# A three-layer fp32 block on one core: where layer 1's convolution, key chains and gates stand among the attention units

## The chip, the cores and the metric

One Trainium2 chip, one core. The time is device microseconds of one launch, the median over the runs. All arithmetic is fp32; in the third layer it is fp32 split into two fp32r parts.

## The reference, cut to what matters

Sequence 256, model width 1024, 256 memory tokens. An even layer (0), an odd layer (1) and a third layer of another kind, which the change doesn't touch. Layer 1:

```python
h = rms_norm(x, norm_g)
c_a, c_b, c_g, d_q, d_kv, d_bg, d_g, m_q, m_g = split_cols(h @ w_in, ODD_SPLITS)
# conformer_conv: 31 taps per channel over 512 channels, causal
y = conv(pad(c_a * sigmoid(c_b))) + conv_b
y_c = silu(rms_norm(y, c_norm)) * silu(c_g)
# nsa: 8 heads; each softmax(q k) v over 15 compressed keys ("cmp"),
# over the selected blocks ("slc") and over the window ("win"), weighted by gates
kc = rope(rms_norm(compress(k_cmp_raw), knorm))     # 15 keys, an MLP over 32 tokens each
y_d = nsa(d_q, kv, gates, ...) * silu(d_g)
# memory_attention: 4 heads over 256 memory tokens, q and k normed
y_m = memory_attention(m_q, mem_n, m_wkv, ...) * silu(m_g)
x = x + concat([y_c, y_d, y_m]) @ w_out
```

Layer 0 has the same memory attention, an 8-head differential attention (two softmaxes a head) and a gated unit, with q and k normed per group and turned by rope.

## The kernel before, in words

The kernel writes each engine's instruction stream by hand; each stream is executed in order, and engines meet at semaphores. TensorE (PE) does projections, transposes, scores and values. ScalarE (ACT) copies projections out of PSUM, does exp and tanh, and copies turned probabilities out. VectorE (DVE) does norms, rope, masks, row maxima, the scaling of probabilities, and most of the convolution. GpSimd (POOL) does the power of each norm (L1905, one small instruction per norm, in the order of the list `NORMS`), one of the four channel tiles of the convolution, and in the third layer the low parts of the weights (L1873). SyncE loads weights in the order of `WHOLE`, five slots deep.

A projection of 512 columns (`project`, L452) has two halves; each fills one of two PSUM banks (the ring `proj`). Transposes go through another two banks (the ring `xpose`), in the order of `xpose_names`; a turn waits until the bank's last content has been copied out.

Attention is cut into units, one softmax of one head over all 256 queries: layer 0 has 20 (4 memory, 16 differential), layer 1 has 28 (4 memory, then cmp, slc, win for each of 8 heads). `layer_units` is a software pipeline with the same iteration i on every engine. TensorE: scores of unit i+1 (L558), some steps of the "fill" projections (L452), turn of unit i-1 (L568), values of unit i-2 (L575). VectorE: logits and row minimum of unit i (`unit_logits`, L1411 to L1421), probabilities of unit i-1 (`unit_probs`, L1428 to L1434), finished fill pieces, and then `extra(i)`. ScalarE: exp of unit i, tanh of a fill piece, copy of unit i-1.

The fill of layer 1 is `L1_FILL = ["c_b", "c_a", "c_g", "d_g"]`, 64 steps spread over the 28 units. So the convolution's input is there only at about unit 14. From then on VectorE does 6 taps of the convolution at the end of every iteration (3 channel tiles x 2 taps, L1608 and L1610; only every third waits for its result) and GpSimd 31 taps of the fourth tile (L1884 to L1888, a product and a sum each). After the last unit come, in order: the last taps, bias (L1629), transposes (L748), the turns of `ym1` and of `yb1` (from y_d), `out_rest` (the output projection's last 256 rows) and the first part of `out_project`, then the turn of `ya1` (from y_c), the rest, and the residual. The norm of y_c and its gate run beside `out_rest`.

Ahead of the units, layer 1 projects `d_q`, `dkv1`, `dkv2`, runs the 128 small matmuls of the compression (L691), projects `m_qg1`, and then goes through two short chains with every engine in turn: hidden layer, `kvc`, norm and rope of the compressed keys, `kc`; and norm and turn of the memory queries (`mq1`).

Of the kernel before, what the change touches and what calls it, by code (L numbers as in the profile page):

```python
# [10 lines left out]
ALU = mybir.AluOpType  # L11
# [52 lines left out]
L1_FILL = ["c_b", "c_a", "c_g", "d_g"]  # L64
# [7 lines left out]
def both(names):  # L72
# [4 lines left out]
WHOLE = (both(["kv0", "b_q", "b_k", "m_qg0", "b_v"] + L0_FILL) + out_halves(0)  # L77
         + both(["kv1", "d_q", "dkv1", "dkv2", "cmp_w1", "m_qg1"] + L1_FILL) + out_halves(1))
# [94 lines left out]
FILL_MM = 4 * T * KT  # L173


def fill_after(i, n):

    return min(FILL_MM, FILL_MM * (i + 1) // n)


def pieces_at(i, n):

    before = fill_after(i - 1, n) // KT if i else 0
    return range(before, fill_after(i, n) // KT)


def xpose_names():
    out = [f"mem{j}" for j in range(4)] + [f"x0_{j}" for j in range(4)]
    out += ["mk0", "q0", "q1", "k0", "k1", "mq0"]
    out += [("unit", i) for i in range(len(UNITS0))]  # L190
    out += ["z0", "z1", "ym0", "ya0_0", "ya0_1", "yb0_0", "yb0_1"]
    out += [f"x1_{j}" for j in range(4)] + ["cmp", "dq0", "dq1", "hid_k", "hid_v", "mk1", "dk0", "dk1", "hid_t", "kvc", "kc", "mq1"]
    out += [("unit", len(UNITS0) + i) for i in range(len(UNITS1))]
    out += ["yc0", "yc1", "ym1", "yb1_0", "yb1_1", "ya1_0", "ya1_1"]
    out += [f"x2_{j}" for j in range(4)] + ["rq0", "rq1", "rk0", "rk1"] + [("ret", h) for h in range(RET_HEADS)]
    out += [f"ret_y{j}" for j in range(4)] + [f"x3_{j}" for j in range(4)]
    return out


def proj_names():  # L200
    out = []
    for b in ["kv0", "b_q", "b_k", "m_qg0", "b_v"] + L0_FILL + ["out0"] + \
# [11 lines left out]
def build(nc, early_d, late_d, positions_d, x_d, mem_d, blocks_d, out_d):  # L214
# [5 lines left out]
    with ExitStack() as ctx:  # L220
# [62 lines left out]
        kc_rows = logits[:, 1, 0:256].rearrange("p (g c d) -> p g c d", g=2, d=64)  # L283
# [18 lines left out]
        def pair_of(c0, i):  # L302
# [30 lines left out]
        normed = Milestones(sem("normed"), ["mem", "x0", "mk0", "q", "k", "mq0", "a_v", "y_m0", "y_a0", "y_b",  # L333
                                               "x1", "dq", "mk1", "dk", "hid", "kc", "mq1", "conv", "y_m1",
                                               "y_d", "y_c", "x2", "rq", "rk", "g_ret", "x3"])
        NORMS = [("mem", 2), ("x0", 2), ("mk0", 8), ("q", 32), ("k", 32), ("mq0", 8), ("a_v", 8),
                 ("y_b", 16), ("x1", 2), ("dq", 16), ("mk1", 8), ("dk", 8), ("kc", 2), ("mq1", 8), ("y_c", 2), ("x2", 2), ("gn0", 4), ("gn1", 4),
# [8 lines left out]
                              [(1, "tanh", p) for p in range(4, 8)])  # L346
# [42 lines left out]
        def slot_left(eng, part):  # L389
            if part > 0:  # L390
                last = max(j for j in whole_done if j % WHOLE_SLOTS == part - 1)
                eng.wait_ge(*whole_done[last])
            else:
                eng.wait_ge(*whole_done[whole_index[("kv1", 1)]])
# [15 lines left out]
        CONV_FROM = 1 + max(i for i in range(len(UNITS1)) if 3 in pieces_at(i, len(UNITS1)))  # L410
        CONV_VECTOR, CONV_POOL = (0, 1, 2), 3
# [8 lines left out]
        def _(pe):  # L420
# [75 lines left out]

            def turn_pair(name, tiles):
# [9 lines left out]
            def out_rest(layer):  # L507
# [5 lines left out]
                for c in range(4):  # L513
# [3 lines left out]
                    for t in range(T):  # L517
                        for k in range(2):
                            mm = products(psum[:, bank + ring.slot(use), t * HC:(t + 1) * HC],
                                          pick(h_whole, slice(None), k, slice(t * P, (t + 1) * P)),  # L520
# [70 lines left out]
            turned(pe, "x0_2", "x0_3")  # L591
            project("b_q", h_whole)
            normed.wait(pe, "mk0")
            turn_pair("mk0", lambda a, t: mkv[:, 0, t, a * P:(a + 1) * P])
            project("b_k", h_whole)
# [3 lines left out]
            project("m_qg0", h_whole)  # L599
            normed.wait(pe, "k")  # L600
            for j in range(2):
                turn_pair(f"k{j}", lambda a, t: rows[:, t, 2048 + (2 * j + a) * P:2048 + (2 * j + a + 1) * P])
            project("b_v", h_whole)
            normed.wait(pe, "mq0")
            turn_pair("mq0", lambda a, t: rows[:, t, 3584 + a * P:3584 + (a + 1) * P])
            turned(pe, "k0", "k1", "mq0")
            turned(pe, "q0", "q1", "mk0")
            chunk_read(pe, "b_v")
# [12 lines left out]
            def layer_units(units, base, operands, fill, group_starts):  # L621
                filler = (s for name in fill for t in range(T)
                          for s in (features_piece if name in ("c_a", "c_b") else rows_piece)(name, t, h_whole))
# [4 lines left out]
                for i in range(n + 2):  # L628
                    if i + 1 < n:
                        unit_scores(base + i + 1, units[i + 1], *operands(units[i + 1])[0:2])  # L630
                    while issued < fill_after(i, n):
# [4 lines left out]
                    if i >= 2:  # L636
                        if i - 2 in group_starts:
                            heads_out.wait(pe, group_starts[i - 2])
                        unit_values(base + i - 2, units[i - 2], *operands(units[i - 2])[2:])
                for _ in filler:  # L640
                    pass


            layer_units(UNITS0, 0, operands0, L0_FILL, {4: "mem0"})
# [35 lines left out]
            for j in range(2):  # L680
                turn_pair(f"dq{j}", lambda a, t: rows[:, t, (2 * j + a) * P:(2 * j + a + 1) * P])
            project("dkv2", h_whole, (HC, 24))
            src_full.wait(pe, "cmp")
# [14 lines left out]
            normed.wait(pe, "mk1")  # L698
            turn_pair("mk1", lambda a, t: mkv[:, 1, t, a * P:(a + 1) * P])
            normed.wait(pe, "dk")  # L700
            for j in range(2):
                turn_pair(f"dk{j}", lambda a, t: rows[:, t, 3072 + (2 * j + a) * P:3072 + (2 * j + a + 1) * P])
            project("m_qg1", h_whole)
# [6 lines left out]
            turned(pe, "hid_t")  # L710
            xpose.claim(pe, "kvc")
            for c in range(2):
                for g in range(2):
                    at = (2 * c + g) * 64
                    mm = nc.tensor.matmul(psum[0:N_CMP, XPOSE_BANK + xpose.slot("kvc"), at:at + 64],
                                          hid[:, c, g * N_CMP:(g + 1) * N_CMP], E("cmp_w2")[:, c * 64:(c + 1) * 64],
                                          start=True, stop=True)
            fill(xpose, mm, "kvc")
            normed.wait(pe, "kc")
            xpose.claim(pe, "kc")  # L720
            for g in range(2):
                mm = nc.tensor.transpose(psum[:, XPOSE_BANK + xpose.slot("kc"), g * 16:(g + 1) * 16],
                                         kc_rows[0:16, g].rearrange("p a d -> p (a d)"), ident[0:16, 0:16])
            fill(xpose, mm, "kc")
            normed.wait(pe, "mq1")
            turn_pair("mq1", lambda a, t: rows[:, t, 1536 + a * P:1536 + (a + 1) * P])
            turned(pe, "dq0", "dq1", "mk1", "dk0", "dk1", "kc", "mq1")
# [15 lines left out]
            layer_units(UNITS1, len(UNITS0), operands1, L1_FILL, {0: "diff", 4: "mem1"})  # L743
            normed.wait(pe, "conv")
            for t in range(T):
                xpose.claim(pe, f"yc{t}")
                for f in range(4):
                    mm = nc.tensor.transpose(psum[:, XPOSE_BANK + xpose.slot(f"yc{t}"), f * P:(f + 1) * P],  # L748
                                             conv_out[:, f, t * P:(t + 1) * P], ident)
                fill(xpose, mm, f"yc{t}")  # L750
            normed.wait(pe, "y_m1")
            turn_pair("ym1", lambda a, t: rows[:, t, 1792 + a * P:1792 + (a + 1) * P])
            normed.wait(pe, "y_d")
            for j in range(2):
                turn_pair(f"yb1_{j}", lambda a, t: rows[:, t, 2560 + (2 * j + a) * P:2560 + (2 * j + a + 1) * P])
# [8 lines left out]

            def project_features(name, src):
                for half in range(2):
                    for _ in features_piece(name, half, src):
                        pass
# [127 lines left out]
        def _(act):  # L896
# [119 lines left out]
            act.wait_ge(lam_exp, 1)  # L1016
            copy_chunk("b_q", rows[:, :, 1536:2048])
            copy_chunk("b_k", rows[:, :, 2048:2560])
            copy_chunk("m_qg0", rows[:, :, 3584:4096])

            gate_m.mark(nc.scalar.activation(gate_tmp[:, :, :], rows[:, :, 3840:4096], ACT.Tanh, scale=0.5), 0, act)
            copy_chunk("b_v", rows[:, :, 2560:3072])

            def fill_half(layer, p, name, gelu):

                arrive(proj, name)
                if layer == 1 and p < 2:

                    proj.freed(nc.scalar.activation(rows[:, p, 3584:4096], bank_of(name),
                                                    ACT.Tanh, scale=0.5), name, act)  # L1030
                    return
                if layer == 1 and p < 4:
                    return
# [998 lines left out]
```

## Time and profile before

| | us |
|---|---|
| median of 3 runs | 1113.35 (1112.9 to 1115.66) |
| the profiled execution | 1114.8 |
| its span | 1113.0 |
| PE busy | 962.0 (86%) |
| DVE busy | 465.6 (42%) |
| ACT busy | 362.1 (33%) |
| POOL busy | 537.6 (48%) |

Layer 0's first score is at 98.47 us of the span, layer 1's first score at 353.68, and layer 1's output projection begins at 511.45; the third layer's work takes the rest from about 564. A row of a timeline gives start, duration, engine, line, operation, out<-in, shapes, the number of merged instructions, and in brackets the idle time before it and who ended it.

### The profile page before, as it was taken

Reading aid. Unit: us, or ns where it says so; the run is one execution under the profiler, and the core shown is the slowest. Engines: PE = TensorE matmul, PEld = TensorE weight load, DVE = VectorE, ACT = ScalarE, POOL = GpSimd, SP = SyncE. Lnnn points to the kernel's source line nnn. Section 1 sums busy time; section 2 is a strip of 40 time slices with the busy share of each in tenths; the row PEclk is TensorE's granted clock in tenths of the full one; section 3 lists DMA queues with packets and bytes.
Section 4 is the critical chain, followed back from the end, with each engine's and each line's share of the span. In section 5 each row is a group of like instructions: output and inputs, shape, how many; then the busy total and the mean of one; then the engine's idle time right before and its main releaser. Section 6 shows DMA issues by size and latency. Waiting matters only on the chain.

```text
span 1113.0 us, 15392 instructions
## 1 busy us (share of the span) xinstructions
PE 962.0 (86%) x5960; PEld 864.6 (78%) x5960; DVE 465.6 (42%) x965; ACT 362.1 (33%) x641; POOL 537.6 (48%) x710
## 2 busy tenths in 40 slices
PE   4999799999995996878789887769998699999995
PEld 3888578788884874657689877669998699899994
DVE  1454545421334459985189330560113236222231
ACT  2212333301001432222144474524433434334441
POOL 0030000000110029400469949379889578999993
PEclk9999899999997997797989898979999799999998
DMA  8343122233442221132234434135454335555551
GB/s 324 124 143 116 73 76 76 77 125 140 151 152 76 76 76 39 39 113 90 67 99 149 143 112 152 61 108 187 156 171 152 114 133 170 172 186 178 185 181 47
DMA packets 37608, 139.36 MB, mean 125 GB/s; under 512 B 4256, under 2 KB 4256, under 8 KB 37280
## 3 DMA queue, kind: packets, MB, share of 16 engines
q1 hardware_dynamic: 37392, 136.97, 36.2%
q10 hardware_dynamic: 144, 1.41, 0.3%
q8 instruction: 47, 0.77, 0.3%
q14 instruction: 25, 0.20, 0.1%
HBM read 137.32 MB, written 1.05 MB: 124 GB/s over the span
## 4 chain that ended last, share of the span: by engine, by line
PE 21%; POOL 19%; DVE 5%; ACT 4%; issue 1%; DVEq 0%; ACTq 0%; POOLq 0%
POOL w_lo L1873 18%; PE psum L453 7%; PE psum L454 7%; PE psum L455 7%; DVE y_lo L1276 1%; ACT w_hi L910 1%; DVE h_lo L1250 0%; PE psum L504 0%; DVE h_rows L1752 0%; ACT act_tmp L966 0%; POOL rstd L1905 0%; ACT h_hi L933 0%; ACT y_hi L961 0%; ACT rows L1148 0%; ACT rows L1146 0%
## 5 line engine op out<-in xcount | busy, mean ns | idle before, releaser
L1873 POOL TENSOR_TENSOR w_lo<-raw,w_hi 128x256 fp32r<-128x256 f32 x624 | 460.0, 779 | 106.5 <-ACT w_hi L910 65.4
L452 PE MATMUL psum<-w_whole,h_whole 128*128 128x256 f32 (+1 forms) x960 | 224.3, 391 | 2.2 <-ACT h_whole L945 2.2
L1905 POOL TENSOR_TENSOR rstd<-mean_sq,minus_half 128x2 f32<-128x2 f32 (+4 forms) x20 | 34.1, 1704 | 395.0 <-DVE mean_sq L1288 395.0
L453 PE MATMUL psum<-h_hi,w_hi 128*128 128x256 f32 x704 | 204.8, 291 | 20.8 <-POOL w_lo L1873 16.7
L452 PEld LDWEIGHTS psum<-w_whole,h_whole 128*128 128x128 f32 x960 | 183.1, 197 | 37.2 <-issue 10.2
L454 PE MATMUL psum<-h_lo,w_hi 128*128 128x256 f32 x704 | 203.6, 289 | 0.0
L455 PE MATMUL psum<-h_hi,w_lo 128*128 128x256 f32 x704 | 203.3, 289 | 0.0
L910 ACT ACTIVATE w_hi<-raw 128x1024 fp32r<-128x1024 f32 x156 | 159.0, 1054 | 108.3 <-DMA raw<-in_blocks 63.8
L453 PEld LDWEIGHTS psum<-h_hi,w_hi 128*128 128x128 f32 x704 | 139.8, 199 | 23.2 <-issue 18.3
L454 PEld LDWEIGHTS psum<-h_lo,w_hi 128*128 128x128 f32 x704 | 140.0, 199 | 0.0
L455 PEld LDWEIGHTS psum<-h_hi,w_lo 128*128 128x128 f32 x704 | 139.7, 198 | 0.0
L984 ACT ACTIVATE logits<-logits,neg_max 128x128 f32<-128x128 f32 (+2 forms) x96 | 41.4, 431 | 93.1 <-DVE neg_max L1421 57.0
L453 PE MATMUL psum<-w_hi,h_hi 128*128 128x256 f32 x192 | 56.7, 295 | 12.4 <-DVE rows L1770 6.2
L453 PE MATMUL psum<-w_hi,y_hi 128*128 128x512 f32 (+1 forms) x160 | 56.8, 355 | 4.3 <-DVE y_lo L1276 3.6
L452 PE MATMUL psum<-w_whole,y_whole 128*128 128x256 f32 x256 | 56.1, 380 | 1.9 <-DVE y_whole L1259 1.9
L568 PE MATMUL psum<-early,logits 128*128 128x128 f32 (+1 forms) x144 | 26.3, 294 | 35.5 <-DVE logits L1434 35.4
L454 PE MATMUL psum<-w_lo,y_hi 128*128 128x512 f32 (+1 forms) x160 | 56.3, 352 | 0.0
L455 PE MATMUL psum<-w_hi,y_lo 128*128 128x512 f32 (+1 forms) x160 | 56.2, 351 | 0.0
L454 PE MATMUL psum<-w_lo,h_hi 128*128 128x256 f32 x192 | 56.0, 292 | 0.0
L455 PE MATMUL psum<-w_hi,h_lo 128*128 128x256 f32 x192 | 55.9, 291 | 0.0
L452 PEld LDWEIGHTS psum<-w_whole,y_whole 128*128 128x128 f32 x256 | 48.5, 190 | 8.8 <-ACT y_whole L942 2.3
L568 PEld LDWEIGHTS psum<-early,logits 128*128 128x128 f32 (+1 forms) x144 | 17.6, 144 | 46.5 <-DVE logits L1434 43.0
(264 smaller groups left out, 1421.4 us busy)
## 6 DMA issues: line engine op xcount, KB each, us to landing
raw<-in_blocks SPq DMA_DIRECT2D x156, 512.0 KB, 3.4
w_whole<-in_blocks SPq DMA_DIRECT2D x96, 512.0 KB, 4.4
early<-in_early SPq DMA_DIRECT2D x1, 1647.0 KB, 8.4
attention<-in_late ACTq DMA_DIRECT2D x1, 1380.0 KB, 5.8
rows<-in_mem SPq DMA_DIRECT2D x1, 1024.0 KB, 4.9
x<-in_x SPq DMA_DIRECT2D x1, 1024.0 KB, 10.5
out_x<-h_rows SPq DMA_DIRECT2D x1, 1024.0 KB, 4.0
positions<-in_positions SPq DMA_DIRECT2D x1, 1.0 KB, 10.2
```

Source lines behind the costliest of these rows:

```text
L452: return nc.tensor.matmul(out, lhs[0], rhs[0], start=start, stop=stop, skip_group_check=shared_bank)
L453: nc.tensor.matmul(out, lhs[0], rhs[0], start=start, stop=False, skip_group_check=shared_bank)
L454: nc.tensor.matmul(out, lhs[0], rhs[1], start=False, stop=False, skip_group_check=shared_bank)
L455: return nc.tensor.matmul(out, lhs[1], rhs[0], start=False, stop=stop, skip_group_check=shared_bank)
L568: mm = nc.tensor.transpose(bank[0:rows_, n * P:(n + 1) * P], logits[:, i % 3, u.cols(t, kb)], ident)
L910: nc.scalar.activation(split_part(w_hi, q), raw[:, q % RAW_SLOTS, :], ACT.Copy).then_inc(w_hi_ready, 1)
L984: ins = nc.scalar.activation(logits[:, i % 3, u.seg(t)], logits[:, i % 3, u.seg(t)], ACT.Exp, bias=neg_max[:, i % 2, t:t + 1], scale=-1.0, ...
L1276: src_lo.mark(V.tensor_tensor(pair[1][at], src, pair[0][at].bitcast(F32), ALU.subtract), name, vec)
L1873: ins = nc.gpsimd.tensor_tensor(lo[:, at], full[:, at], hi[:, at].bitcast(F32), ALU.subtract)
L1905: rstd_ready.mark(nc.gpsimd.tensor_tensor(rstd[:, n % 2, 0:width], mean_sq[:, n % 2, 0:width], minus_half[:, 0:width], ALU.pow), name, pool)
```

## The change

- **Layer 0.** `m_qg0` is projected first, the memory queries are normed and turned ahead of b_q, and the turns of k (`k0`, `k1`) move from ahead of the units into iteration 1.
- **Layer 1, order.** `c_b` and `c_a` leave the fill and are projected ahead of `dkv2`; `m_qg1` comes ahead of the compression. `L1_FILL` is `c_g` and `d_g`, 32 steps, spread over 27 units.
- **Convolution.** VectorE has two tiles (1, 3) in place of three, one after the other, each tap waiting for the one before; 24 taps ahead of the units, 3 per iteration from iteration 3. GpSimd has two tiles (0, 2): 20 taps ahead of the power of `mq1`, 6 ahead of that of `kc`, the other 36 ahead of that of `y_c`.
- **Key chain.** `kvc`, the norm of the compressed keys and `kc` move into iterations 1 and 2.
- **End of y_c.** Bias in iteration 17, transposes in 18, norm in 19, tanh in 20, gate in 21, turns of `ym1` and `ya1` in 22. After the units only y_d is left; `out_project` begins with the rows of y_c.

```diff
-L1_FILL = ["c_b", "c_a", "c_g", "d_g"]
+L1_FILL = ["c_g", "d_g"]
+CONV_END = 17
+FILL_UNITS = [20, 27]
-    out += ["mk0", "q0", "q1", "k0", "k1", "mq0"]
-    out += [("unit", i) for i in range(len(UNITS0))]
+    out += ["mk0", "mq0", "q0", "q1", ("unit", 0), "k0", "k1"]
+    out += [("unit", i) for i in range(1, len(UNITS0))]
-            ["kv1", "d_q", "dkv1", "dkv2", "m_qg1"] + L1_FILL + ["out1"] + \
+            ["kv1", "d_q", "dkv1", "c_b", "c_a", "dkv2", "m_qg1"] + L1_FILL + ["out1"] + \
-        CONV_VECTOR, CONV_POOL = (0, 1, 2), 3
+        CONV_VECTOR, CONV_POOL = (1, 3), (0, 2)
...
# TensorE, layer 1
+            project_features("c_b", h_whole)
+            normed.wait(pe, "mk1")
+            turn_pair("mk1", ...)
+            normed.wait(pe, "dk")
+            for j in range(2):
+                turn_pair(f"dk{j}", ...)
+            project_features("c_a", h_whole)
             project("dkv2", h_whole, (HC, 24))
+            project("m_qg1", h_whole)
             src_full.wait(pe, "cmp")
...
+            normed.wait(pe, "mq1")
+            turn_pair("mq1", ...)
             normed.wait(pe, "hid")
...
+            def between_units(i):
+                if i == 1:
+                    turned(pe, "hid_t")
+                    xpose.claim(pe, "kvc")
...
+                elif i == 2:
+                    normed.wait(pe, "kc")
...
+                    turned(pe, "kc")
+                elif i == CONV_END + 1:
+                    normed.wait(pe, "conv")
...
+                elif i == CONV_END + 5:
+                    normed.wait(pe, "y_c")
+                    turn_pair("ym1", ...)
+                    for j in range(2):
+                        turn_pair(f"ya1_{j}", ...)
             out_rest(1)
-            turned(pe, "yb1_0", "yb1_1")
-            out_project(1, range(4, 8), lambda: turn_last(3584, "y_c", ("ya1_0", "ya1_1")))
+            turned(pe, "ya1_0", "ya1_1")
+            out_project(1, range(0, 4), lambda: turn_last(2560, "y_d", ("yb1_0", "yb1_1")))
# VectorE, layer 1: each half of c_a, then 8 taps; later, ahead of the hidden layer, 8 more
+            for half in range(2):
...
+                proj.freed(ins, ("c_a", half), vec)
+                taps(8)
...
+            normed.mark(grouped_norm("mq1", heads(rows, 1536, 4, 64), E("m1_qnorm")), "mq1", vec)
...
+            taps(8)
             for j, name in enumerate("kv"):
                 arrive(xpose, f"hid_{name}")
...
             def extra1(i):
+                if 3 <= i < CONV_END:
+                    taps(3)
+                if i == 1:
+                    arrive(xpose, "kvc")
...
+                elif i == CONV_END:
+                    taps(2 * 31)
+                    vec.wait_ge(conv_sums, len(CONV_POOL))
...
+                elif i == CONV_END + 2:
+                    grouped_norm("y_c", yc, E("c_norm")).then_inc(yc_normed, 1)
...
# GpSimd
+                for half, f in enumerate(CONV_POOL):
+                    proj.read(pool, ("c_a", half))
+                    for tap in range(31):
...
+            taps_ahead = {"mq1": 20, "kc": 6, "y_c": 2 * 31}
             for n, (name, width) in enumerate(NORMS):
-                if name == "y_c":
...
+                for _ in range(taps_ahead.get(name, 0)):
+                    next(conv, None)
```

## Rows read from the trace of the kernel before

**Rows 1.** Busy time of the engines by stretch: width, busy time (instructions), granted clock

```profile
353.60:410.90 57.30, 57.22 (x305) 46.92 (x306) 26.58 (x91) 21.35 (x73) 0.00 (x0) 0.95 0.18 57
410.90:458.90 48.00, 34.01 (x139) 25.17 (x137) 45.73 (x82) 9.35 (x34) 43.23 (x61) 0.82 0.14 48
458.90:500.00 41.10, 31.21 (x152) 24.11 (x153) 36.39 (x105) 11.94 (x41) 0.00 (x0) 0.90 0.25 89
500.00:511.40 11.40, 7.92 (x35) 6.93 (x35) 8.02 (x17) 2.67 (x5) 0.00 (x0) 0.50 0.31 124
```

**Rows 2.** TensorE timeline at the start of layer 0's units

```profile
96.86 0.60 PE L504 MATMUL psum<-early,rows 128*128 128x128 f32 x4
98.47 1.14 PE L558 MATMUL psum<-attention 64*128 64x256 f32 x8 [1.00 <-DVE attention L1330]
```

**Rows 3.** TensorE timeline ahead of layer 1's units

```profile
303.83 10.56 PE L452 MATMUL psum<-w_whole,h_whole 128*128 128x256 f32 x64
314.31 8.87 PE L691 MATMUL psum<-w_whole,h_rows 64*30 64x128 f32 x128
326.06 13.98 PE L452 MATMUL psum<-w_whole,h_whole 128*128 128x256 f32 x64
...
345.90 0.39 PE L722 MATMUL psum<-early,logits 16*128 16x16 f32 x2 [4.28 <-DVE logits L1573]
350.93 1.12 PE L504 MATMUL psum<-early,rows 128*128 128x128 f32 x4 [4.63 <-DVE rows L1304]
353.68 2.08 PE L558 MATMUL psum<-attention 64*128 64x256 f32 x8 [1.63 <-DVE attention L1330]
```

**Rows 4.** GpSimd timeline, layer 1: norms, first and last convolution instruction

```profile
347.64 1.64 POOL L1905 TENSOR_TENSOR rstd<-mean_sq,minus_half 128x8 f32<-128x8 f32 x1 [3.84 <-DVE mean_sq L1288]
410.92 0.61 POOL L1884 TENSOR_TENSOR h_rows<-rows,early 128x256 f32<-128x256 f32 x1 [61.64 <-DVE rows L1594]
...
458.13 0.72 POOL L1888 TENSOR_TENSOR h_rows<-h_rows,rope_tmp 128x256 f32<-128x256 f32 x1
```

**Rows 5.** VectorE convolution taps by form: without GpSimd, then beside it

```profile
L1610 DVE SCALAR_TENSOR_TENSOR h_rows<-rows,early,h_rows 128x256 f32<-128x256 f32 x6 | 2.6, 481 | 0.1
...
L1610 DVE SCALAR_TENSOR_TENSOR h_rows<-rows,early,h_rows 128x256 f32<-128x256 f32 x6 | 4.8, 847 | 0.1
```

**Rows 6.** VectorE timeline: starts of iterations 15, 18, 21 and 24

```profile
417.95 0.56 DVE L1414 SCALAR_TENSOR_TENSOR logits<-psum,early 128x384 f32<-128x384 f32 x1
...
441.71 0.56 DVE L1414 SCALAR_TENSOR_TENSOR logits<-psum,early 128x384 f32<-128x384 f32 x1
...
463.25 0.56 DVE L1414 SCALAR_TENSOR_TENSOR logits<-psum,early 128x384 f32<-128x384 f32 x1
...
477.03 0.56 DVE L1414 SCALAR_TENSOR_TENSOR logits<-psum,early 128x384 f32<-128x384 f32 x1
```

**Rows 7.** TensorE timeline: turns of units 7 and 10

```profile
386.24 0.49 PE L568 MATMUL psum<-early,logits 128*128 128x128 f32 x3
...
397.81 0.49 PE L568 MATMUL psum<-early,logits 128*128 128x128 f32 x3
```

**Rows 8.** VectorE timeline: compressed keys and memory queries

```profile
341.74 0.41 DVE L1566 TENSOR_SCALAR kvc<-psum 15x256 f32<-15x256 f32 x1 [0.79 <-PE psum L715]
...
345.38 0.22 DVE L1572 COPY logits<-kvc 15x128 f32<-15x128 f32 x1
...
347.33 0.17 DVE L1288 TENSOR_SCALAR mean_sq<-sumsq 128x8 f32<-128x8 f32 x1
```

**Rows 9.** VectorE and TensorE timeline after the last unit

```profile
503.68 1.14 DVE L1629 TENSOR_SCALAR h_rows<-h_rows,early 128x256 f32<-128x256 f32 x4
...
512.49 1.23 DVE L1297 TENSOR_TENSOR scratch<-rows 128x1024 f32<-128x1024 f32 x1
...
517.33 1.29 DVE L1304 SCALAR_TENSOR_TENSOR rows<-rows,early 128x512 f32<-128x512 f32 x2
...
511.45 7.56 PE L452 MATMUL psum<-w_whole,h_whole 128*128 128x256 f32 x32
```

More of the change, by code:

```diff
@@ L73, in both @@
     return [(n, h) for n in names for h in range(2)]
[L77 to L78 removed]
+WHOLE = (both(["kv0", "m_qg0", "b_q", "b_k", "b_v"] + L0_FILL) + out_halves(0)
+         + both(["kv1", "d_q", "dkv1", "c_b", "c_a", "dkv2", "m_qg1", "cmp_w1"] + L1_FILL) + out_halves(1))
 HALVES = (both(["x_lru0", "x_lru1", "r_q", "r_k", "y_lru0", "y_lru1", "lru_w", "r_v0", "r_v1", "g_ret0", "g_ret1"]
@@ L598, in _ @@
                 turn_pair(f"q{j}", lambda a, t: rows[:, t, 1536 + (2 * j + a) * P:1536 + (2 * j + a + 1) * P])
[L599 to L602, printed above, removed]
             project("b_v", h_whole)
[L604 to L608, printed above, removed]
+            turned(pe, "mk0", "mq0", "q0", "q1")
             chunk_read(pe, "kv0")
@@ L619, in operands0, with layer_units @@
                         u.sub == 0, u.sub == 1)
-            def layer_units(units, base, operands, fill, group_starts):
-                filler = (s for name in fill for t in range(T)
-                          for s in (features_piece if name in ("c_a", "c_b") else rows_piece)(name, t, h_whole))
+            def layer_units(layer, units, base, operands, fill, group_starts, extra=lambda i: None):
+                filler = (s for name in fill for t in range(T) for s in rows_piece(name, t, h_whole))
                 n = len(units)
@@ L697, in _ @@
                 ends(("cmp_w1", half), *full_value(xpose, "hid_v"))
[L698 to L703, printed above, removed]
+            normed.wait(pe, "mq1")
+            turn_pair("mq1", lambda a, t: rows[:, t, 1536 + a * P:1536 + (a + 1) * P])
             normed.wait(pe, "hid")
@@ L709, in _ @@
             fill(xpose, mm, "hid_t")
[L710 to L727, printed above, removed]
+            turned(pe, "dq0", "dq1", "mk1", "dk0", "dk1", "mq1")
             chunk_read(pe, "kv1")
@@ L1046, in fill_tanh, with layer_units @@
                               (layer, "tanh", p), act)
-            def layer_units(layer, units, base, fill, groups):
+            def layer_units(layer, units, base, fill, groups, extra=lambda i: None):
                 n = len(units)
@@ L1083, in _ @@
             copy_chunk("dkv1", rows[:, :, 512:1024])
+            for half in range(2):
+                arrive(proj, ("c_b", half))
+                proj.freed(nc.scalar.activation(rows[:, half, 3584:4096], bank_of(("c_b", half)), ACT.Tanh, scale=0.5),
+                           ("c_b", half), act)
             copy_chunk("dkv2", rows[:, :, 1024:1304], (HC, 24))
@@ L1558, in _ @@
             normed.mark(V.memset(lam_tmp[:, 7:8], 0.0), "hid", vec)
-            turn_in("mk1", mk_t[:, 1])
-            for j in range(2):
-                turn_in(f"dk{j}", k_t[:, 2 * j:2 * j + 2, :])
+            turn_in("mq1", mq_t[:, :, :])
             arrive(xpose, "hid_t")
```

334 lines of the change are left out of this document (177 added, 157 removed).

## The prediction, before the changed kernel ran

> **What bounds the kernel now.** I read the page's chain of waits first: it stays in the third layer, which the change doesn't touch and which waits for the second residual, so whatever layers 0 and 1 gain or lose passes on to the end. Then busy time by stretch [rows 1]. From 353.6 to 410.9 TensorE has no idle time (57.2 of 57.3 us at clock 0.95): it bounds. From 410.9 to 458.9 VectorE is busy 45.7 of 48.0 us and TensorE 34.0 at a granted clock of 0.82: VectorE bounds, since convolution taps stand in every iteration. Up to 500 VectorE still leads (36.4 of 41.1), and from 500 to 511.4 short transposes follow the last unit at clock 0.50. The change puts work and waits of these last two stretches elsewhere, and takes on the 10.5 us of waits ahead of the units (4.28, 4.63 and 1.63) [rows 3].
>
> Two prices from VectorE decide. A tap lasts 481 ns with GpSimd idle, and six go by in 2.6 us; beside GpSimd's taps it lasts 847 ns, and six take 4.8, that is 0.81 each [rows 5]. GpSimd does 31 taps in 47.9 us, 1.55 each [rows 4]: two instructions per tap, so one VectorE tap per GpSimd instruction. Three iterations with 18 taps take 23.8 us beside GpSimd (417.95 to 441.71) and 13.8 without (463.25 to 477.03) [rows 6]. Without the taps (14.5 and 7.8 us) and one fill piece (0.9, in the first only), three iterations cost VectorE 8.4 us beside GpSimd and 5.9 without.
>
> **Layer 0.** TensorE waits 1.00 us for the memory queries after a 0.60 turn [rows 2]; with q, k and mq in the new order VectorE's k norm ends with `b_v`, and I get the first score at 97.1 in place of 98.5. The two k turns (2 x 0.5) come back in iteration 1, and `k1` needs the bank that ScalarE has to empty of unit 0 (about 0.6). Net +0.3, bounds -1.4 and +2.
>
> **Layer 1 up to the units.** c_b starts where `dkv2` did, at 303.8. TensorE then runs 13.98 (c_b), 2.0 (mk1 and dk turns), 13.98 (c_a), 10.5 (dkv2), 13.98 (m_qg1), 8.9 (compression) [rows 3]: it ends at 367.0. c_a's first half is there at 326.8, GpSimd starts at 328.1 and has 20 taps by 359.1, in time for `mq1`, whose sums are ready at 360.8 (m_qg1 ends at 358.1). GpSimd's power takes 1.64 [rows 4], so 362.7; then GpSimd starts 6 more taps. VectorE finishes norm and gate, slowed by them, at 366.7, and now has 8 taps ahead of the hidden layer: 6.5 us, 373.2. TensorE's turn of `mq1` wants the bank of `hid_k`, which VectorE frees behind those taps: TensorE idles from 367.0 to about 373.4, and wakes on the low clock. From the `mq1` turn to the first score took 2.75 us before (350.93 to 353.68) [rows 3]: first score at 376.1, +22.4. So of 28 us of projections moved ahead, 5.6 are paid by waits that went; a new wait of 6 us replaced the rest.
>
> **Iterations 0 to 3.** Two of them begin as before (logits 0 at 378.2, probabilities 0 done at 382.0). Iteration 1 then has the whole key chain inside VectorE's stream: 4.1 us before (341.7 to 345.8) [rows 8], with a memset 4.4, and once GpSimd has its power it resumes the last 36 taps (at 385.8) and the small two-input operations behind it wait for its instructions, some eight times 0.3: 391. Unit 1's turn and `kc` wait for that; iteration 2 ends at 396, iteration 3 with its 3 taps at 400.9. Before, iteration 4 began at 367.5: the shift is now +33.4.
>
> **Iterations 4 to 16.** GpSimd ends at 385.8 + 36 x 1.55 = 441.9. Beside it an iteration costs 8.4/3 + 3 x 0.81 = 5.2 us (before: 6 taps, 7.6); 40.1 us without one piece give 7.7 of them. TensorE's own work is 2.9: three units took 11.57 [rows 7], of which 28 instructions of fill at 13.98/64 = 0.218 (6.1 us), so 1.8 a unit, and 1.0 of fill now. The remaining 4.3 iterations with taps cost 2.0 + 3 x 0.52 = 3.5 (each tap now waits for the one before, so 481 ns and an issue of 35): with one piece, iteration 16 begins at 457.3, iteration 17 at 458.8. Before, it began at 433.1: +25.7.
>
> **Iteration 17 to the output projection.** Bias 1.1 [rows 9]; VectorE waits about 2 for the transposes and copies 1.4; the norm of y_c is 6.2 in one piece (512.49 to 518.6 [rows 9]), in iteration 19, in which TensorE idles some 5 us; gate 2.5; the three turns of iteration 22 cost VectorE about 4 us of waiting, because three bank uses are emptied one by one. Eleven iterations of VectorE's 1.97 make 21.6, its y_c work 11.9, two pieces 1.6, and the waits about 14 (2 and 4 above, 5 in iterations 24 to 27 where TensorE's 2.9 bounds, 3 for the last values): 49.4. `out_rest` starts at 508.2, not 511.45: -3.3. It no longer needs y_d, whose product and copy (3 us) lie under 14 us of matmuls, as y_c's gate did.
>
> **Sum.** +0.3 - 3.3 = -3.0 on a span of 1113.0. The profiled execution took 1114.8, above the median of 1113.35; I take the difference off the median: **1110.4**. The third layer is the same work from the residual on. `late` loads earlier, hidden; the weights' queue keeps its five slots, and its last loads wait for fill that ends at 500 and are needed after 535.
>
> **GpSimd's lock.** On the traces GpSimd loses little to VectorE: 1.55 a tap with VectorE busy 45.7 of 48 us [rows 1, 4]. The Trainium skill (SBUF — State Buffer, Who interferes with whom) says that a VectorE instruction with two SBUF inputs and a GpSimd instruction that reads SBUF hold the shared pair for the whole instruction, and the other fully blocks. By this rule, GpSimd would lose a tap's whole 0.48 each time too; the sum without the rule stands above, and what it would do is the third rival.
>
> **Rivals.**
> - *Lighter contention (faster).* With two tiles each, VectorE's taps fall between GpSimd's instructions and cost 0.52, the lower bound of rows 5. Then the hidden layer comes 2.4 us earlier, an iteration beside GpSimd costs 4.3, 9.3 fit instead of 7.7, worth 5.6 us: 1102. For it speaks that a tap with nothing beside it needs only that; against it, that beside GpSimd all six taps of a row pay 0.81.
> - *Each tap misses a turn (slower).* All of VectorE's taps now wait for the one before; before, two in three didn't. If a tap that comes late lets GpSimd through again, it costs up to two GpSimd instructions, 1.55. The taps ahead of the hidden layer cost 6 more, an iteration 7.4, so 5.4 fit and 2.3 more run at 3.5 (+8): 1125. The gain is gone at 0.95 a tap and the kernel slower by 0.3% at 1.1. Against: a GpSimd instruction of 0.6 to 0.8 is much longer than the 35 ns of issue.
> - *GpSimd is held up (slower).* If VectorE's two-input operations block it fully, about 1.8 of each 5.2 us, its 36 taps take 85 us: they end at 471, VectorE waits in iteration 17, and the end is 12 later: 1123.
> - *The wait only moves (no change).* TensorE at clock 0.8 or below has 5.5 us of work per iteration at the low level against VectorE's 5.2; three idle stretches of 5 us or more each bring that level. 3 us lost so: 1113.
>
> **Numbers.** Chances: the forecast 0.50 (its own range 1106 to 1115), lighter contention 0.17, missed turns 0.12, GpSimd held up 0.05, the wait only moves 0.16. What this kernel's measurement can tell from no change is about 0.3%, 3.3 us; 1110.4 lies just inside it. The forecast's half splits 0.27 faster, 0.21 same, 0.02 slower. With the rivals: faster 0.44, same 0.37, slower 0.19. Range: 1102 from the lighter contention to 1120, between the forecast and the two slow rivals.
>
> **What the changed profile would show.** First score of layer 0 near 97.1. A hole in TensorE of about 6 us ahead of the `mq1` turn, ended by VectorE; first score of layer 1 near 376. VectorE's taps at about 0.85 until GpSimd's last one near 442, and 0.48 after; iterations of 5.2 and 3.5 us. No wait of VectorE for GpSimd in iteration 17. A TensorE hole of 5 us in iteration 20. `out_rest` at 508, then 37 us as before. I am wrong if taps cost another price, if GpSimd ends later than 455, or if TensorE's low clock makes it the bound beside GpSimd.

## The result, and the profile after

The changed kernel took 1127.7 us (median of 4, 1125.7 to 1129.0) against 1114.3 for the kernel before (4 runs beside it): a ratio of 1.0116, 95% interval 1.010 to 1.0131. It is slower by 1.2%, 13 us; I had forecast 1110.4, and 1120 was the upper end. The profiled execution took 1125.7, its span is 1123.9 (before: 1113.0), so the rows below hold 10.9 us of the loss.

Busy time by stretch of the changed kernel, the columns as in [rows 1]. The columns are start and end, width, then busy time with instructions of TensorE, of its weight loads, of VectorE, ScalarE and GpSimd, then TensorE's granted clock (1.00 is 2.4 GHz, 0.50 is 1.2 GHz), the DMA engines' busy share and GB/s. The stretches run from the first score to iteration 4, to GpSimd's last tap, to iteration 17, to the end of TensorE's wait for y_c's norm, through the three turns, to `out_rest`.

```profile
375.60:402.60 27.00, 18.00 (x74) 13.61 (x74) 17.95 (x36) 6.16 (x19) 16.34 (x25) 0.63 0.00 1
402.60:439.60 37.00, 31.60 (x118) 23.36 (x118) 34.57 (x68) 10.09 (x37) 33.31 (x48) 0.64 0.08 29
439.60:462.60 23.00, 20.66 (x96) 15.60 (x94) 18.67 (x57) 8.63 (x31) 0.61 (x1) 0.80 0.13 47
462.60:484.00 21.40, 15.48 (x82) 11.94 (x83) 14.69 (x39) 5.30 (x19) 0.71 (x1) 0.90 0.15 50
484.00:499.50 15.50, 15.19 (x61) 11.83 (x61) 7.13 (x17) 6.07 (x17) 0.00 (x0) 0.61 0.00 0
499.50:518.30 18.80, 14.74 (x88) 12.14 (x87) 10.65 (x39) 7.94 (x27) 0.00 (x0) 0.95 0.35 130
```

Two things stand out. Before, TensorE had no idle time in the 57 us after its first score, at clock 0.95 [rows 1]. Now it idles 9.0 of the first 27 us, and its granted clock is 0.63 (between the 1.2 and the 2.4 GHz level, nearer the lower). And from 484 to 499.5 it is busy all the time (15.19 of 15.5) at 0.61: there the clock itself costs time.

TensorE's timeline of the changed kernel: the first scores of both layers, the three places in layer 1 where it idled over 4 us, and `out_rest`; these answer to [rows 2, 3, 9]:

```profile
95.56 1.14 PE L566 MATMUL psum<-attention 64*128 64x256 f32 x8 [0.45 <-DVE q_t L1350]
...
373.24 1.09 PE L512 MATMUL psum<-early,rows 128*128 128x128 f32 x4 [8.00 <-DVE scratch L1623]
375.66 2.08 PE L566 MATMUL psum<-attention 64*128 64x256 f32 x8 [0.98 <-DVE hid L1629]
...
393.46 1.11 PE L576 MATMUL psum<-early,logits 128*128 128x128 f32 x4 [8.36 <-DVE logits L1458]
...
483.97 0.59 PE L576 MATMUL psum<-early,logits 128*16 128x128 f32 x2 [5.19 <-DVE logits L1458]
...
518.29 9.62 PE L455 MATMUL psum<-w_whole,mem_t 128*128 128x256 f32 x32
```

All three holes end with VectorE. Its timeline shows with what it was busy: the 8 taps; the key chain (its first instruction, two of its small two-input ones, and its last, a copy); its wait for the turn of `kc`; then iteration 4, the first after GpSimd's last tap, and iteration 17 (in iteration 11, three taps in 1.53 us):

```profile
366.36 6.42 DVE L1587 SCALAR_TENSOR_TENSOR h_rows<-rows,early,h_rows 128x256 f32<-128x256 f32 x8
...
383.09 0.41 DVE L1642 TENSOR_SCALAR kvc<-psum 15x256 f32<-15x256 f32 x1 [1.45 <-PE psum L751]
...
387.47 0.70 DVE L1338 TENSOR_TENSOR scratch<-kvc,early 15x16 f32<-15x16 f32 x1
388.21 0.16 DVE L1339 TENSOR_TENSOR kvc<-scratch 15x16 f32<-15x16 f32 x1
...
389.77 0.65 DVE L1651 COPY scratch<-kvc 15x128 f32<-15x128 f32 x1
...
396.60 0.19 DVE L1654 COPY kc_t<-psum 128x32 f32<-128x32 f32 x1 [3.20 <-PE psum L759]
...
402.64 0.19 DVE L1438 SCALAR_TENSOR_TENSOR logits<-psum,early 128x32 f32<-128x32 f32 x1
...
440.52 0.56 DVE L1438 SCALAR_TENSOR_TENSOR logits<-psum,early 128x384 f32<-128x384 f32 x1
...
442.64 1.53 DVE L1587 SCALAR_TENSOR_TENSOR h_rows<-rows,early,h_rows 128x256 f32<-128x256 f32 x3
...
462.63 0.56 DVE L1438 SCALAR_TENSOR_TENSOR logits<-psum,early 128x384 f32<-128x384 f32 x1 [1.30 <-issue]
```

VectorE itself waits in the stretch behind: for the transposes of y_c, for the three turns of iteration 22, and for the tanh of the last fill piece:

```profile
472.74 1.42 DVE L1670 COPY rows<-psum 128x512 f32<-128x512 f32 x2 [2.75 <-PE psum L768]
...
498.80 0.69 DVE L1279 TENSOR_SCALAR y_whole<-psum 128x512 f32<-128x512 f32 x1 [6.89 <-PE psum L512]
...
511.60 0.69 DVE L1471 SCALAR_TENSOR_TENSOR rows<-act_tmp,psum 128x512 f32<-128x512 f32 x1 [3.40 <-ACT act_tmp L1052]
```

GpSimd: end of its taps ahead of the keys' power, the power, its last tap; these answer to [rows 4]:

```profile
371.72 0.78 POOL L1929 TENSOR_TENSOR h_rows<-h_rows,rope_tmp 128x256 f32<-128x256 f32 x1
384.46 0.71 POOL L1943 TENSOR_TENSOR rstd<-mean_sq,minus_half 128x2 f32<-128x2 f32 x1 [11.96 <-DVE mean_sq L1308]
...
439.42 0.79 POOL L1931 TENSOR_TENSOR h_rows<-h_rows,rope_tmp 128x256 f32<-128x256 f32 x1
```

### The profile page after: what moved, and what is told of

The parts are those of the page before. It is cut to its first block and busy times, and to the rows that moved or that the text cites. A ratio compares the mean times of both kernels' runs of the same rounds, so it can differ in the third digit from the quotient of the medians.

```text
span 1123.9 us, 15419 instructions
## 1 busy us (share of the span) xinstructions
PE 974.5 (87%) x5960; PEld 873.8 (78%) x5960; DVE 461.7 (41%) x934; ACT 362.3 (32%) x641; POOL 580.2 (52%) x771
## 5 line engine op out<-in xcount | busy, mean ns | idle before, releaser
L455 PE MATMUL psum<-w_whole,h_whole 128*128 128x256 f32 (+1 forms) x928 | 228.0, 403 | 2.2 <-ACT h_whole L963 2.2
L455 PEld LDWEIGHTS psum<-w_whole,h_whole 128*128 128x128 f32 x928 | 180.3, 202 | 41.8 <-issue 15.0
L576 PE MATMUL psum<-early,logits 128*128 128x128 f32 (+1 forms) x144 | 28.7, 316 | 38.4 <-DVE logits L1458 38.3
L994 ACT ACTIVATE rows<-psum 128x512 f32<-128x512 f32 (+1 forms) x24 | 13.9, 580 | 130.6 <-PE psum L455 110.4
## 6 DMA issues: line engine op xcount, KB each, us to landing
positions<-in_positions SPq DMA_DIRECT2D x1, 1.0 KB, 10.1
```

Source lines behind the costliest of these rows:

```text
L455: return nc.tensor.matmul(out, lhs[0], rhs[0], start=start, stop=stop, skip_group_check=shared_bank)
L576: mm = nc.tensor.transpose(bank[0:rows_, n * P:(n + 1) * P], logits[:, i % 3, u.cols(t, kb)], ident)
L994: proj.freed(nc.scalar.activation(dst[:, :, c], bank_of((name, half)).rearrange("p (t n) -> p t n", t=T)[:, :, 0:cols[half]], ACT.Copy), ( ...
```

## The experiments

**Theory A:** the loss is VectorE work put where TensorE has nothing else left: the 8 taps ahead of the hidden layer, the key chain in iteration 1, the norm of y_c in iteration 19. **Theory B:** the contention between VectorE's and GpSimd's taps, each of which runs longer while the other engine works. **Theory C:** TensorE's low clock.

| run | us, median | ratio to before, 95% interval |
|---|---|---|
| the change | 1127.7 | 1.0116 (1.0100 to 1.0131) |
| layer 0's part alone | 1113.7 | 0.9990 (0.9977 to 1.0004) |
| y_c's end behind the units | 1119.9 | 1.0037 (1.0020 to 1.0055) |
| GpSimd's taps left out | 1114.1 | 0.9996 (0.9984 to 1.0009) |
| idle matmuls added | 1124.2 | 1.0086 (1.0067 to 1.0105) |
| 8 taps away from the hidden layer | 1119.5 | 1.0052 (1.0033 to 1.0071) |
| keys ahead of the units | 1123.9 | 1.0091 (1.0067 to 1.0115) |
| y_c's end and the 8 taps, both | 1111.6 | 0.9972 (0.9960 to 0.9983) |
| kernel before, tiles split 2 and 2 | 1117.3 | 1.0035 (1.0021 to 1.0049) |
| reordered | 1106.0 | 0.9929 (0.9912 to 0.9947) |
| reordered, more taps ahead | 1100.3 | 0.9856 (0.9840 to 0.9872) |
| the same with idle matmuls | 1100.8 | 0.9873 (0.9859 to 0.9886) |

Differences between runs are taken from the ratios, times 1114.3; by the intervals such a difference is uncertain by 2 to 3 us. Starts in a trace vary as well: the changed kernel and its variants share their layer 0, and yet layer 1's first projection starts between 302.33 and 305.86 us (302.39 in the changed kernel). Where starts of two traces are compared below, that difference is taken off.

**Layer 0's part alone**, on the kernel before:

```diff
-    out += ["mk0", "q0", "q1", "k0", "k1", "mq0"]
-    out += [("unit", i) for i in range(len(UNITS0))]
+    out += ["mk0", "mq0", "q0", "q1", ("unit", 0), "k0", "k1"]
+    out += [("unit", i) for i in range(1, len(UNITS0))]
```

> The kernel before with the layer 0 part alone. In the changed kernel's trace layer 0's first score came 2.9 us earlier, two thirds of it were lost again in iteration 1, and layer 1 began 1.4 us earlier. Every theory of the loss puts it in layer 1, so here the time should be 1 to 2 us below that of the kernel before (ratio 0.998 to 1.000). If it is above 1.002, part of the 13 us comes from layer 0.

1.1 us faster, and the interval holds no change as well: layer 0 has no part in the loss.

**y_c's end behind the units.** The norm, tanh, gate and turns of y_c and the turn of `ym1` stand after the last unit as in the kernel before; the convolution's end stays in iteration 17.

```diff
-                elif i == CONV_END + 2:
-                    grouped_norm("y_c", yc, E("c_norm")).then_inc(yc_normed, 1)
...
             source("yb1_1", y_whole[0][:, 6:8, :], 0.5)
+            grouped_norm("y_c", yc, E("c_norm")).then_inc(yc_normed, 1)
```

> The changed kernel with the norm, tanh, gate and turns of y_c and the turn of y_m put back after the last unit, beside the output projection as before; bias and transposes stay in iterations 17 and 18. Theory A (work of VectorE that was hidden beside the output projection now stands between units, with TensorE idle 5.2 and then on the low clock): about 12 us of VectorE leave the units, 3 to 4 us of waiting for y_d and the turns come back after them, so 8 to 11 us less than the changed kernel, 1117 to 1120. Theory B (GpSimd's two tiles slow every iteration up to the eleventh): the end of y_c is a small part, at most 4 us less, 1124 or more.

8.8 us come back (the single runs lie between 1115.4 and 1121.8), as Theory A had it. The last stretches of this kernel, in the columns of the first fence:

```profile
462.60:484.00 21.40, 20.68 (x103) 15.96 (x101) 12.48 (x43) 7.13 (x27) 0.00 (x0) 0.86 0.11 31
484.00:499.50 15.50, 14.99 (x87) 11.88 (x87) 8.82 (x35) 7.30 (x29) 0.00 (x0) 1.00 0.07 27
```

In the same 15.5 us TensorE does 87 instructions in place of 61, at clock 1.00 in place of 0.61. The hole of 5.19 and the 6.89 are gone.

**GpSimd's taps left out.** The two tiles of GpSimd are filled with zeros, so 62 taps of the convolution are not computed.

> The changed kernel without GpSimd's convolution: its two channel tiles are left out (zeros in their place), so nothing of GpSimd stands beside VectorE's taps. Theory B: VectorE's taps cost 0.52 in place of 0.81 and its other two-input operations lose 0.8 us an iteration; the hidden layer comes 3 us earlier and eight iterations cost 3.5 in place of 5.2: 14 to 17 us less than the changed kernel, 1111 to 1114. Theory A: no more than these iterations can give before TensorE's low clock bounds them: 5 to 9 us less.

13.4 us less, as much as the whole loss, at the edge of what Theory B expected (14 to 17) and above Theory A's 5 to 9. A tap of VectorE lasts 485 ns, the hole ahead of the `mq1` turn is 3.97 us, the one behind the keys 4.92: the contention is in the length of the very pieces that Theory A names. From 402.6 to 439.6 TensorE is now busy 34.4 of 37 us, at clock 0.72, and VectorE 26.0: with the contention gone TensorE is next. This does not show that the change lost by contention. The kernel before has it too [rows 5], no run took GpSimd's taps out of that one, and here the work of 62 taps is not moved but gone.

**Idle matmuls.** Six matmuls of the unit matrix ahead of the wait for the probabilities in iterations with units 4 to 12 and two to sixteen in those up to 21; their product is overwritten.

```diff
-                pe.wait_ge(probs_ready, i + 1)
...
+                for _ in range(WARM.get(i - len(UNITS0), 0)):
+                    nc.tensor.matmul(bank[:, 3 * P:4 * P], ident, ident, start=True, stop=True)
+                pe.wait_ge(probs_ready, i + 1)
```

> The changed kernel with added matmuls of the identity into unused PSUM columns while TensorE waits for probabilities (6 in each of units 4 to 12, 2 in 13 to 18, 16 in 19, 4 in 20 and 21), 0.21 us each at the high level, 0.43 at the low. Theory C (TensorE fell to the low level, clock 0.61 to 0.64 in three stretches, and then bounded iterations 12 to 27 and the first 10 us of the output projection): the granted clock from 402 to 440 rises above 0.85 and the time falls by 3 to 7 us, to 1121 to 1125. Without an effect of the clock the added work costs 0 to 6 us: 1128 to 1134.

3.3 us less, hardly more than the intervals leave open. Where they come from, in the columns of the first fence (its second, third and fifth stretch):

```profile
404.40:441.90 37.50, 34.50 (x183) 28.77 (x183) 34.91 (x68) 10.09 (x37) 33.81 (x48) 0.82 0.09 29
441.90:466.20 24.30, 22.93 (x150) 19.78 (x149) 18.20 (x57) 8.63 (x31) 0.11 (x1) 0.97 0.12 44
...
487.00:499.00 12.00, 11.69 (x78) 9.84 (x77) 7.47 (x18) 5.92 (x16) 0.00 (x0) 1.00 0.00 0
```

and VectorE's wait for the turns:

```profile
497.93 0.69 DVE L1282 TENSOR_SCALAR y_whole<-psum 128x512 f32<-128x512 f32 x1 [3.17 <-PE psum L513]
```

Iterations 4 to 17 take 61.8 us with the higher clock, 60.0 without: there it buys nothing, and the added matmuls cost 1.8. It buys the turns: VectorE's wait for them is 3.17 in place of 6.89, and from iteration 17 to `out_rest` 52.0 in place of 55.7.

**The 8 taps spread.**

```diff
-            taps(8)
             for j, name in enumerate("kv"):
                 arrive(xpose, f"hid_{name}")
...
-                if 3 <= i < CONV_END:
+                if i < CONV_END and i != 1:
                     taps(3)
```

> The changed kernel with the 8 VectorE taps taken from ahead of the hidden layer, and three each put into iterations 0 and 2 instead. Theory A (those taps are TensorE's hole of 8.0 us ahead of the memory queries' turn): the hole shrinks to 1 to 3 us and the first score of layer 1 comes at 369 to 371 in place of 375.66. The key chain's hole of 8.36 us stays, with 2.4 us of taps ahead of it, so iteration 4 starts at 398 to 400 in place of 402.6, and the time is 1122 to 1125 us. Rival (VectorE has this much work in the stretch up to iteration 4 wherever it stands): iteration 4 still starts at 402 or later, and the time is 1126 to 1129 us.

7.1 us less, more than Theory A expected (1122 to 1125 us). TensorE's holes in this kernel:

```profile
367.81 0.63 PE L512 MATMUL psum<-early,rows 128*128 128x128 f32 x4 [1.55 <-DVE scratch L1622]
369.92 1.14 PE L566 MATMUL psum<-attention 64*128 64x256 f32 x8 [1.25 <-DVE hid L1628]
...
388.60 1.12 PE L576 MATMUL psum<-early,logits 128*128 128x128 f32 x4 [6.48 <-DVE logits L1458]
```

Iteration 4 starts at 397.25; from the start of layer 1 that is 6.4 us earlier, though VectorE has only two taps fewer up to there. The three taps in iteration 2 cost nothing: they lie where VectorE had waited 3.20 us for the turn of `kc` (0.77 now), and the iteration lasts 6.4 us in both traces. Those in iteration 0 cost 1.8 us.

**The key chain ahead of the units again.** `kvc`, `kc` and VectorE's norm and rotation behind `hid_t`, nothing else moved.

> The changed kernel with the key chain (products, norm, rotation, turn) finished ahead of the first unit again. Theory A (the chain costs TensorE the same wherever it stands, since nothing else is left to do for TensorE): the first score comes 7 to 10 us later, the 8.36 us hole behind unit 1 is gone, iteration 4 starts within 2 us of 402.6, the time is 1125 to 1130 us. Rival (the place inside the units' loop is what costs): iteration 4 starts 4 us or more earlier, the time is 1118 to 1123 us.

2.8 us less, no more than the intervals leave open, and neither expectation had it (1125 to 1130 and 1118 to 1123). Iteration 4 starts at 401.77; from the start of layer 1 that is 2.1 us earlier, where Theory A had within 2 and the rival 4 or more. The hole of 8.00 stays and one of 7.50 stands ahead of the `kc` turn; the 8.36 is gone. Moving this chain into the loop was no gain, and a loss of 2 to 3 us at most.

**Both undone**, y_c's end and the 8 taps:

> The changed kernel with two of its placements undone at once: the 8 VectorE taps away from ahead of the hidden layer (three each in iterations 0 and 2), and the y_c norm, gate and turns behind the last unit. Alone they took 0.0064 and 0.0079 off the ratio to the kernel before (7.1 and 8.8 us). If the two losses are separate, the ratio is 1.0116 - 0.0143 = 0.997, 1110 to 1113 us where the kernel before takes 1114. If they overlap (both were the one wait for VectorE), it is 1.000 to 1.004, 1114 to 1119 us.

16.0 us less; the single ones add up to 15.9. The two losses are separate, as far as 2 to 3 us allow. What is left of the change is faster than the kernel before by 3 us, about the gain that I had forecast for the whole of it; that this number is the same is luck, since the forecast counted both pieces in.

**The split of tiles alone**, on the kernel before:

```diff
-        CONV_VECTOR, CONV_POOL = (0, 1, 2), 3
+        CONV_VECTOR, CONV_POOL = (0, 1), (2, 3)
```

> The kernel before with one part of the change: GpSimd takes two of the four convolution tiles in place of one, VectorE two in place of three (4 taps an iteration in place of 6); nothing else is moved. GpSimd then has 62 taps of 1.55 us from 410.9 on, and ends at about 507 in place of 458. Theory A (a GpSimd tap costs 1.5 to 1.6 us and a VectorE tap beside it 0.8, whatever the split): VectorE waits for GpSimd in front of the bias, which comes 3 to 5 us later than at 503.68, and the time is 1116 to 1120 us against 1114.5. Rival (fewer VectorE taps make the iterations so much shorter that TensorE gets through the units sooner and only the wait is late): 1112 to 1116 us.

3.9 us more, inside Theory A's range. GpSimd's last tap starts at 504.56 (before 458.13 [rows 4]), and the bias at 505.66 in place of 503.68 [rows 9]. Until then all of VectorE's taps pay the price of contention; before, those after 458 did not. Of the 2.0 us between the two bias rows, 1.0 is there already at the start of layer 1 (304.82, before 303.83 [rows 3]), so the trace shows less of this cost than the runs' times do.

**A reordered version.** c_b, c_a, compression, `m_qg1`, then `kvc`, `dkv2`, `kc`, `mq1`; y_c's end behind the units.

```diff
-["kv1", "d_q", "dkv1", "c_b", "c_a", "dkv2", "m_qg1"]
+["kv1", "d_q", "dkv1", "c_b", "c_a", "m_qg1", "dkv2"]
-CONV_END = 17
+CONV_END = 13
```

> A version made from the changed kernel: the y_c end behind the last unit (as in the run that moved it), and ahead of the units TensorE does c_b, c_a, compression, m_qg1 (the hidden layer's turn between its halves), the keys' products, dkv2, the keys' and the memory queries' turns; 26 VectorE taps lie beside these projections, 20 of GpSimd's before the keys' power; three taps in each of iterations 0 to 11, the convolution's end in iteration 13. Theory A (the 8.0 and 8.36 us holes and the y_c waits are the loss): no hole over 3 us ahead of or between the first units, first score of layer 1 at 366 to 371, GpSimd's last tap at 426 to 435, out_rest at 490 to 498, time 1097 to 1106 us. Rival (TensorE at its low clock takes most of it back: 28 units of 4 us beside the taps): out_rest at 500 or later, time 1107 to 1114 us.

1106 us, at the upper end of Theory A's range; but `out_rest` came at 501.71, where the rival had put it, so the two theories are not told apart here. The hole ahead of the `mq1` turn was 5.51, not under 3: the keys' chain and the norm of the memory queries take 16 us on VectorE (354.3 to 370.5), the projection over them 10.7. VectorE itself idled 10.6 us in four pieces between 350 and 375 (3.64, 2.36, 1.89 and 2.66).

**The same with these pieces filled** by taps, and the convolution's end one iteration earlier:

```diff
-CONV_END = 13
+CONV_END = 12
...
-            taps(5)
+            taps(9)
             arrive(xpose, "kvc")
...
             turn_in("mq1", mq_t[:, :, :])
+            taps(3)
...
-                    taps(3)
+                    taps(3 - i % 2)
...
-            taps_ahead = {"kc": 20, "mq1": 3, "y_c": 2 * 31}
+            taps_ahead = {"kc": 18, "mq1": 4, "y_c": 2 * 31}
```

> The reordered version with VectorE's idle time ahead of the units filled: 4 more taps ahead of the keys' chain, 3 behind the memory queries' turn, GpSimd's power for the keys after 18 of its taps in place of 20, then 3 and 2 taps by turns in iterations 0 to 11, and the convolution's end in iteration 12. Theory A (beside GpSimd, VectorE's own work sets the pace): an iteration beside GpSimd costs 4.4 to 4.8 us in place of 5.06, iteration 12 starts at 426 to 431 in place of 435.6, out_rest at 494 to 499 in place of 501.7, time 1099 to 1104 us. Rival (TensorE at clock 0.7 is the bound there already): iteration 12 at 433 or later, time 1104 to 1108 us.

> The same kernel, and idle matmuls of the unit matrix (4 in units 0 to 11, 2 in units 12 and 13) while TensorE waits for the probabilities. Theory C (the low granted clock costs time beside the taps): the granted clock from 375 to 430 rises from about 0.7 to 0.8 or more, and the time is 2 to 5 us under the run without them. Rival (VectorE paces these iterations and the clock costs nothing there): within 1.5 us of the run without them.

The first takes 1100.3 us (single runs 1096.1 to 1103.5, the trace is of the longest), 1.4% under the kernel before. The second differs from it by less than the intervals. Both kernels beside the taps, in the columns of the first fence; first without the idle matmuls:

```profile
375.00:425.00 50.00, 44.81 (x162) 32.76 (x162) 46.66 (x84) 15.07 (x51) 45.06 (x65) 0.60 0.06 22
```

and with them:

```profile
375.00:425.00 50.00, 41.11 (x242) 33.45 (x238) 46.65 (x85) 15.56 (x52) 45.06 (x65) 0.93 0.06 22
```

The clock is 0.93 in place of 0.60, TensorE's busy share barely changes, and the first ten iterations take 49.0 us in both (378.01 to 427.01, 376.44 to 425.46). VectorE is busy 46.7 of 50 us in both: it sets the pace. An iteration costs 4.90 us, more than the 4.4 to 4.8 expected. Iteration 12 starts at 435.00, where the rival had put it (433 or later), and `out_rest` at 494.31 and the time are where Theory A had them; this trace starts layer 1 at 305.86, 3.5 us later than that of the reordered version. Theory C is out for this stretch by the second run: the clock rose and the ten iterations did not get shorter.

## Why the prediction was wrong

The step that failed is the waits from iteration 17 to `out_rest`, above all the "about 4 us of waiting" for the three turns of iteration 22: it was 6.89, with TensorE at clock 0.50. Term by term:

**Layer 0:** forecast +0.3, measured a first score at 95.56 in place of 98.47 [rows 2] (forecast 97.1), and nothing that the time shows. Right in what matters.

**Up to the first score of layer 1:** right, and in part by luck. Forecast 376.1, measured 375.66; but the hole ahead of `mq1` was forecast at 6 and measured 8.00, and layer 1 began at 302.39, not at 303.8. The two errors cancel. VectorE is the hole's cause, as said.

**Iterations 0 to 3:** the term was too small by 2.1 us. Iteration 4 forecast at 400.9, measured at 402.64. The key chain takes 7.3 us and ends at 390.42 (forecast 391). Behind it iteration 2 lasts 6.4 us, where 5 were forecast: VectorE waits 3.20 us for the turn of `kc`, while TensorE, behind its hole of 8.36, is at clock 0.50 from 393.4 to 407.

**The taps' price:** right. Forecast 0.81 beside GpSimd and 0.52 alone; measured 6.42 us for 8 (0.80) and 1.53 for 3 (0.51). GpSimd's end forecast 441.9, measured 440.2. Nothing of missed turns; 36 taps of GpSimd from 385.25 to 440.2 are 1.53 each. GpSimd does pay a little. Its two instructions last 0.68 and 0.79 us while VectorE's taps run, and 0.61 and 0.73 when they have ended:

```profile
328.98 0.68 POOL L1927 TENSOR_TENSOR rope_tmp<-rows,early 128x256 f32<-128x256 f32 x1
329.73 0.79 POOL L1929 TENSOR_TENSOR h_rows<-h_rows,rope_tmp 128x256 f32<-128x256 f32 x1
...
352.26 0.61 POOL L1927 TENSOR_TENSOR rope_tmp<-rows,early 128x256 f32<-128x256 f32 x1
352.94 0.73 POOL L1929 TENSOR_TENSOR h_rows<-h_rows,rope_tmp 128x256 f32<-128x256 f32 x1
```

By the rule of the Trainium skill that the prediction cites (SBUF — State Buffer, Who interferes with whom) one side would be fully blocked for the other's whole instruction. This trace doesn't agree: a tap of 0.48 and a GpSimd instruction of 0.61 would then take 1.1 us or more together, and the pair goes by in 0.81. Each pays a part, GpSimd 0.07 us an instruction, VectorE 0.3 us a tap.

**Iterations 4 to 16:** the term was too small by 2.1 us. Forecast 5.2 us beside GpSimd and 3.5 after, measured 5.41 (402.64 to 440.52, 7 iterations) and 3.69 (440.52 to 462.63, 6). Iteration 17 came at 462.63, not 458.8.

**Iteration 17 to `out_rest`:** the step that failed. Forecast "49.4", measured 55.7, the largest part of the 10.1 us by which `out_rest` missed its 508.2. I had priced the wait for the three turns at 4 us at the usual clock; it was 6.89, with TensorE busy all the time at clock 0.50, because the norm of y_c had left it idle for 5.19 just ahead:

```profile
484.00:496.00 12.00, 12.00 (x38) 9.38 (x39) 6.44 (x16) 4.38 (x14) 0.00 (x0) 0.50 0.00 0
496.00:499.50 3.50, 3.19 (x25) 2.45 (x23) 0.69 (x1) 1.68 (x3) 0.00 (x0) 1.00 0.00 0
```

With idle matmuls in that hole the wait is 3.17 and the stretch 52.0, so the clock is 3.7 of the 6.3 us. The other 2.6 are about what VectorE's waits up to the transposes were short of: I had taken "about 2", and it waited 1.84 and 2.75. The hole itself I had forecast, and at its length; that TensorE would then be slow in the turns I had not. Nor had I set the new place of y_c's end against the old one: there the 6.2 us norm and the gate lay beside `out_rest` and cost nothing. Put back, norm, gate and turns together give 8.8 us.

**Behind `out_rest`:** forecast "then 37 us as before", measured 39.3; so 2.1 us are lost, all in `out_rest`, which lasts 9.62 in place of 7.56 [rows 9]. Just ahead of it the clock is 0.55 now and was 0.50 before; over its own length it is 0.73 now and was 0.93. Another 2.0 us are lost in the third layer (from the x2 turns to the end of the span 558.4 us, before 556.4), which I had forecast as the same work. In the reordered version it is 556.4 too; what makes the difference was not tried.

**The rivals.** "The wait only moves" had the right mechanism, three holes and a low clock, in the wrong place: I put the cost of the clock into iterations 4 to 16, where VectorE paces and it costs nothing, and took 3 us for it. "Each tap misses a turn" gave the nearest time, 1125, by a mechanism that the rows exclude, and "GpSimd is held up" 1123, with GpSimd's end at 471, not 440: both numbers are near by luck. "Lighter contention" fell with the price of 0.81. Of the signs that I had named for being wrong (another price, GpSimd later than 455, the low clock as the bound beside GpSimd) none came: the loss lay where I had set no sign.

**The sum by its parts.** The 10.1 us at `out_rest` are -0.4 (first score), +2.1 (to iteration 4), +2.1 (to iteration 17), +6.3 (to `out_rest`); behind it come 4.1. Every forecast but the first was too low, since I priced stretches by busy time plus the waits that I could name. Three of its sums also don't come out as written: 385.8 + 36 x 1.55 is 441.6, not 441.9; the last iteration before the 17th at 2.0 us gives 459.3, not 458.8; and 21.6, 11.9, 1.6 and 14 make 49.1, not 49.4. None is over 0.5 us. What I took as the change's gain, the convolution done early, was there: without the two misplaced pieces of VectorE's work it is 0.3% faster than before, and in the reordered version with VectorE's idle time filled 1.4%.

## What to carry to other kernels

When work of the pacing engine is moved, ask of each piece what the other engines still have to do beside it: here eight taps ahead of a chain of single steps cost 7 us, and six of them spread over iterations little. A large norm that lies beside 14 us of matmuls should not be moved in among short units because it "can be done early"; here that cost 8.8 us with its gate and turns. And in these runs a low clock cost time only where TensorE paced; read that from which engine the waits end with, before spending work on raising it.

## What the runs showed of the hardware

- VectorE's smallest two-input instructions pay the same wait as its large ones beside GpSimd: in the key chain a 15x16 operation takes 0.16 us or 0.70 (388.21 and 387.47 above). The whole chain of small ones, with a memset, goes from 4.5 us (the run without GpSimd's taps, 382.46 to 386.96) to 7.3.
- It is not only instructions with two tensor inputs that pay. The scaling of probabilities, one 128x256 tensor and a scalar per row, takes 0.62 us for two while GpSimd is idle and 1.23 beside its taps; the chain's last copy takes 0.65 beside them and 0.21 in the run without them.

```profile
381.02 0.62 DVE L1458 TENSOR_SCALAR logits<-logits,row_inv 128x256 f32<-128x256 f32 x2
...
392.17 1.23 DVE L1458 TENSOR_SCALAR logits<-logits,row_inv 128x256 f32<-128x256 f32 x2
```

- TensorE was granted 0.60 to 0.64 in stretches in which it was busy 85 to 98% of the time with short matmuls and waits between them. 6 idle matmuls an iteration raised that to 0.82, 4 in the reordered version to 0.93.
- After the hole of 5.19 us TensorE was granted 0.50 through 12 us of continuous work (484 to 496), and 1.00 only then. After those of 8.00 and 8.36 us it was 0.50 too, to 380 and to 407.
